# Hybrid encoder trunk on one core: fills stopped in the keys, grouped logarithms, an earlier split of a read-out, whole high parts

## The reference, cut to what matters

```python
xn = rms_norm(x, norm_mix_pre)
ca, cb, cc, cg = split(xn @ w_in)                    # columns of A, B, C and of three gates
h_a = mlstm(ca)                                      # A: matrix memory, 4 heads, chunks
h_b = sliding_window_attention(cb)                   # B: 8 query heads, window 128
h_c = rwkv7(cc)                                      # C: below
g = sigmoid(cg)
merged = g[0] * (h_a @ w_branch_a) + g[1] * (h_b @ w_branch_b) + g[2] * (h_c @ w_branch_c)
x = x + rms_norm(merged @ w_out, norm_mix_post)
gate, up = split(rms_norm(x, norm_ffn_pre) @ w_ffn_in)
x = x + rms_norm((silu(gate) * up) @ w_ffn_out, norm_ffn_post)
```

```python
w = -softplus(-(w0 + tanh(wl) @ w_w2)) - 0.5; decay = exp(-exp(w))
a = sigmoid(a0 + al @ w_a2)
kk = k * k_k / max(sqrt(sum((k * k_k) ** 2)), 1e-12); k = k * (1 + (a - 1) * k_a)
S = S * decay + (S @ -kk) (kk * a)^T + v k^T;  y = S @ r           # token by token
y = (y - mean(y)) * rsqrt(var(y) + GN_EPS) * gn_g + gn_b           # the read-out
y = (y + sum(r * k * r_k) * v) * (sigmoid(gl) @ w_g2)
```

## Time and profile before

| | |
|---|---|
| device time, median of 3 runs | 2463.97 us (2463.54 to 2465.94) |
| the profiled execution | 2466.26 us, its span 2464.5 us |
| granted TensorE clock, mean | 0.976 |
| busy time of TensorE | 2336.3 us (95% of the span) |
| busy time of VectorE | 997.6 us (40%) |
| busy time of ScalarE | 901.3 us (37%) |
| busy time of GpSimd | 786.4 us (32%) |
| table loads on ScalarE | 69, of 1283 ns each, 88.5 us |
| bytes moved | 180.82 MB, mean 73 GB/s |

### The profile page before, as it was taken

How to read it: one execution, slowest core, us unless ns; L and a number is a source line. 1 busy time by engine, 2 the same in 40 slices (tenths; PEclk the granted TensorE clock), 3 DMA queues, 4 the chain that set the end, 5 groups by cost and what they waited for, 6 DMA issues and landing times.

```text
span 2464.5 us, 53615 instructions
## 1 busy us (share of the span) xinstructions
PE 2336.3 (95%) x23450; PEld 2225.3 (90%) x23450; DVE 997.6 (40%) x1559; ACT 901.3 (37%) x1751; POOL 786.4 (32%) x630
## 2 busy tenths in 40 slices
PE   7999989999899899999989999999998989999997
PEld 7998888888789899999989988888887989999997
DVE  4426654455434522320073276545444534332102
ACT  4345532213354522222344455223323444233222
POOL 3332222112235244444324222222112433444441
PEclk9999989999999999999999999999999999999998
DMA  5532211111214132322334221111112242233331
GB/s 162 135 88 65 61 36 32 28 49 32 60 50 143 57 91 86 90 86 86 82 107 130 61 74 48 28 49 32 28 41 63 72 131 61 87 92 89 89 86 52
DMA packets 334193, 180.82 MB, mean 73 GB/s; under 512 B 33528, under 2 KB 330648, under 8 KB 332936
## 3 DMA queue, kind: packets, MB, share of 16 engines
q1 hardware_dynamic: 333776, 177.34, 26.0%
q10 hardware_dynamic: 184, 0.05, 0.0%
HBM read 167.98 MB, written 9.38 MB: 72 GB/s over the span
## 4 chain that ended last, share of the span: by engine, by line
PE 81%; DVE 10%; ACT 4%; issue 3%; DMA 1%; POOL 1%; SPq 0%; DVEq 0%; ACTq 0%; POOLq 0%
PE psum_products L657 72%; PE psum_mixer L657 7%; DMA w_raw<-in_w_in 1%; ACT w_high L1221 1%; DVE xn_low L2047 1%; DVE merged L2041 1%; DVE x L1671 1%; ACT L1221 0%; ACT c_in_rate L1221 0%; DVE squares_ffn L1665 0%; DVE gate_product L2039 0%; POOL w_low L2270 0%; DVE squares L1638 0%; PE psum_mixer L1036 0%; SPq L2118 0%
## 5 line engine op out<-in xcount | busy, mean ns | idle before, releaser
L2270 POOL TENSOR_TENSOR w_low<-w_raw,w_high 128x512 fp32r<-128x512 f32 (+2 forms) x606 | 761.5, 1278 | 1562.4 <-ACT w_high L1221 1561.0
L657 PE MATMUL psum_products<-xn_high,w_high 128*128 128x272 f32 (+1 forms) x3424 | 741.3, 298 | 43.0 <-POOL w_low L2270 14.2
L657 PE MATMUL psum_products<-xn_high,w_low 128*128 128x272 f32 (+1 forms) x3424 | 713.2, 290 | 0.0
L657 PE MATMUL psum_products<-xn_low,w_high 128*128 128x272 f32 (+1 forms) x3424 | 712.1, 290 | 0.0
L657 PEld LDWEIGHTS psum_products<-xn_high,w_high 128*128 128x128 f32 x3424 | 545.1, 190 | 64.2 <-issue 32.8
L657 PEld LDWEIGHTS psum_products<-xn_low,w_high 128*128 128x128 f32 x3424 | 546.1, 191 | 0.0
L657 PEld LDWEIGHTS psum_products<-xn_high,w_low 128*128 128x128 f32 x3424 | 542.8, 191 | 0.0
L1221 ACT ACTIVATE w_high<-w_raw 128x512 fp32r<-128x512 f32 (+2 forms) x606 | 331.2, 595 | 169.8 <-PE psum_products L657 140.1
L657 PE MATMUL psum_products<-hidden_high,w_high 128*128 128x272 f32 x704 | 145.9, 288 | 0.0
L657 PE MATMUL psum_products<-hidden_high,w_low 128*128 128x272 f32 x704 | 145.7, 288 | 0.0
L657 PE MATMUL psum_products<-hidden_low,w_high 128*128 128x272 f32 x704 | 145.1, 288 | 0.0
(11 more groups left out here) (373 smaller groups left out, 2991.7 us busy)
## 6 DMA issues: line engine op xcount, KB each, us to landing
w_raw<-in_w_in SPq DMA_DIRECT2D x112, 512.0 KB, 4.0
w_raw<-in_w_ffn_in SPq DMA_DIRECT2D x88, 512.0 KB, 3.8
w_raw<-in_w_ffn_out SPq DMA_DIRECT2D x32, 512.0 KB, 3.9
w_raw<-in_w_out SPq DMA_DIRECT2D x16, 512.0 KB, 3.9
w_raw<-in_w_ffn_out SPq DMA_DIRECT2D x16, 384.0 KB, 3.3
x_kept<-x SPq DMA_DIRECT2D x2, 2176.0 KB, 7.6
x<-x_kept SPq DMA_DIRECT2D x2, 2176.0 KB, 9.0
w_raw<-in_w_in SPq DMA_DIRECT2D x16, 256.0 KB, 3.8
```

Source lines behind the costliest of these rows:

```text
L657: return pe.matmul(out, lhsT, rhs, start=start, stop=stop, skip_group_check=True)
L2270: low_ready.inc(pool.tensor_tensor(wl[:, n % NSPLIT, ks_], wraw[:, slot, ks_], wh[:, n % NSPLIT, ks_].bitcast(F32), ALU.subtract))
```

## The change

1. `fill` has an argument `on`. With `fill(n, False)` it runs k steps of the next unit only and stops at its end. The three fills of `c_prep`, `c_keys` and `c_scale` are called so. In the plan all units keep their places.
2. The variance step of the read-out writes var with a Copy, and `c_rsqrt` does Ln, two instructions of 128x1090, and then Exp, two of the same size. VectorE's `c_finish` waits at blocks 0 and 2, for one half each.
3. `a_out_split` moves from behind the attention to just ahead of its last step: it now stands between C's column unit 12 and `b_out(8)`.
4. `w_high` is one Copy of up to 128x1024; GpSimd's two subtractions per unit both wait for it.

The diff, cut to its core:

```diff
@@ -163,7 +163,7 @@
 WEIGHT = {"c_prep": 1.0, "c_keys": 1.0, "c_scaled": 0.3, "c_scale": 1.0, "c_gram": 0.7, "c_level": 0.3, "c_chain": 0.5,
-          "c_state_out": 0.0, "a_chunk": 0.6, "a_chunk_out": 0.5, "a_state_out": 0.0, "a_state_put": 0.0, "b_put": 0.0, "c_shift_put": 0.0, "c_state_put": 0.0, "a_scale": 0.3, "a_out": 0.2, "b_values": 0.5,
+          "c_state_out": 0.0, "a_chunk": 0.6, "a_chunk_out": 0.5, "a_out_split": 0.0, "a_state_out": 0.0, "a_state_put": 0.0, "b_put": 0.0, "c_shift_put": 0.0, "c_state_put": 0.0, "a_scale": 0.3, "a_out": 0.2, "b_values": 0.5,
           "b_scores": 0.6, "b_out": 0.6}
@@ -211,13 +211,14 @@
             second += [("b_scores", l, c + 2)] if c < 7 else []
+            second += [("a_out_split", l)] if c == 7 else []
         second = weave(second, [("cols_c", l, j) for j in range(1, CT)])
         plan += second
-        plan += [("a_out_split", l), ("gate", l) + GATES[0], ("c_shift_out", l)]
+        plan += [("gate", l) + GATES[0], ("c_shift_out", l)]
         c = []
@@ -730,10 +731,10 @@
 
-            def fill(steps):
+            def fill(steps, on=True):
 
                 u = unit_at[0]
-                while steps > 0 and u < len(units) and u < unit_at[0] + 2 and fillable(units[u]):
+                while steps > 0 and u < len(units) and u < unit_at[0] + 1 + on and fillable(units[u]):
                     s = units[u]
@@ -822,7 +823,7 @@
 
-                fill(2)
+                fill(2, False)
                 bank[2].claim(pe)
@@ -833,7 +834,7 @@
                 bank[0].filled(to_tokens(0, cc[:, 8:12, at:at + n], nch, L), "act")
-                fill(4)
+                fill(4, False)
 
@@ -846,7 +847,7 @@
             def c_keys(l, g):
-                fill(8)
+                fill(8, False)
 
@@ -1227,8 +1228,8 @@
                 act.wait_ge(landed[at].sem, value)
-                for ks_ in half_blocks(s):
-                    high_ready.inc(fn(wh[:, n % NSPLIT, ks_], wraw[:, unit_no[s] % NRAW, ks_], ACT.Copy))
+                nk = nk_of(s)
+                high_ready.inc(fn(wh[:, n % NSPLIT, 0:nk], wraw[:, unit_no[s] % NRAW, 0:nk], ACT.Copy))
 
@@ -1376,11 +1377,13 @@
                     c0, c1 = (0, Y_CUT) if b == 0 else (Y_CUT, CW)
-                    step(fn(y_rn[:, f, c0:c1], mp[2 + b][:, 0:c1 - c0], ACT.Ln, scale=1.0 / 64, bias=C("scalars", 1, 1)),
-                         bank[2 + b].empty["act"])
+                    step(fn(y_rn[:, f, c0:c1], mp[2 + b][:, 0:c1 - c0], ACT.Copy, scale=1.0 / 64), bank[2 + b].empty["act"])
 
             def c_rsqrt(l):
-                step(fn(y_rn[:], y_rn[:], ACT.Exp, scale=-0.5), flow("c_gn_r"))
+                for f in (0, 2):
+                    step(fn(y_rn[:, f:f + 2, :], y_rn[:, f:f + 2, :], ACT.Ln, bias=C("scalars", 1, 1)))
+                for f in (0, 2):
+                    step(fn(y_rn[:, f:f + 2, :], y_rn[:, f:f + 2, :], ACT.Exp, scale=-0.5), flow("c_gn_r"))
 
@@ -1853,7 +1856,7 @@
 
-                if f == 0:
+                if f % 2 == 0:
                     flow("c_gn_r").wait_next(dve, "dve")
@@ -2266,7 +2269,7 @@
                 for half, ks_ in enumerate(half_blocks(s)):
-                    pool.wait_ge(high_ready.sem, 2 * low_no[n] - 1 + half)
+                    pool.wait_ge(high_ready.sem, low_no[n])
                     low_ready.inc(pool.tensor_tensor(wl[:, n % NSPLIT, ks_], wraw[:, slot, ks_],
```

## The result

| | before | after |
|---|---|---|
| device time, median | 2463.76 us (4 runs, 2462.57 to 2465.94) | 2448.08 us (4 runs, 2445.10 to 2449.73) |
| profiled execution, its span | 2466.26, 2464.5 us | 2449.73, 2447.9 us |
| busy time of TensorE | 2336.3 us | 2335.9 us |
| granted clock, mean of the profiled execution | 0.976 | 0.977 |
| table loads | 69 | 57 |

A forecast was written before the change was run, and what follows sets the result against it. TensorE, busy 95% of the span, bounds the kernel; only its 128 us idle and half-clock time can shrink. Per layer −2.7 + 1.7 − 5.9 + 0 = −6.9; twice, plus 0.5: −13.3 us, so 2450.7 us, range 2437 to 2464.

The forecast's parts named there:

- A: Fills stopping at a unit's end, groups 1 to 4: −2.7 us a layer, +1.7 charged for half clock.
- B: Logarithms grouped in the read-out: fewer table loads and a shorter wait for c_y_squares, −5.9 us a layer.
- C: a_out_split moved inside the attention: new 3.6 us wait against time given back; 0 taken, between −1.5 and +3.5 a layer.
- D: w_high in one Copy: ScalarE wins nothing, GpSimd may begin 0.5 us later; +0.5 us once, at the start.
- 503.4 − 498.4 − 6.0 + 1.5 = +0.5: Group 2: TensorE's arrival less chain end, less eight steps put off, plus two already put off: 0.5 us gained.
- I charge one spell: Waits for c_kprime in groups 1 to 4: one spell of 3.4 us at half clock, costing 1.7 us a layer.
- the three steps put off: Three gate steps now ahead of c_y_squares(1) in the read-out: cut its wait from 0.9 to about 0.4 us.
- that for c_tanh_w shrinks to about 1.2: End of the attention: with the read-out split earlier, TensorE's wait for c_tanh_w shrinks to about 1.2 us.
- But at full clock: Behind the attention: c_tanh_w's matmuls start some 1.6 us later but at full clock, where they took twice their time.
- The first: Rival: the new waits leave the clock alone, −19.7 us, 2444.3 us; chance 0.25.
- The second: Rival: only the table loads count, the other gains go into waits and clock, −1.9 us, 2462 us; chance 0.17.
- the third: Rival: uncovered waits each throw TensorE to 1.2 GHz for 10.2 us, costing 5.1 each; +20.9, 2484.9 us; chance 0.08.

The follow-up runs named there:

- A alone: Only the fills that stop at a unit's end, against the kernel before the change: 2452.02 us, ratio 0.9948.
- C alone: Only the move of a_out_split ahead of the attention's last step, against the kernel before the change: 2468.35 us, ratio 1.0019.
- c_prep only: Only the two fills of c_prep stop at a unit's end, those of c_keys and c_scale go on, against the kernel before the change: 2459.65 us, ratio 0.9982.

## Why the prediction was right, and where it was not

**The total** came out as forecast, but out of terms that were not. Forecast per layer, and measured alone over both layers: A −1.0 with its clock (−2.0 in all), measured −12.8; B −5.9 (−11.8), measured −10.6; C 0, measured +4.7; D +0.5 once, measured +8.4. The measured ones sum to −10.3, where the full change measured −15.3 and −15.7: A and B lose 3 us beside each other, and C and D, which cost 4.7 and 8.4 us alone, cost 5.2 together beside A and B. So the total is right by luck: A was worth far more than forecast, C and D cost what was not forecast, and the parts do not add.

**Part A.** The failed step is "503.4 − 498.4 − 6.0 + 1.5 = +0.5" and its like: it took TensorE's arrival in groups 2 and 4 as fixed, with 2.72 and 3.15 us of waiting for gate_tanh in it. gate_tanh is queued on ScalarE behind the chain that starts 1.5 us sooner, so it came sooner too, and TensorE waits 0.78 and 1.27 us for it after the change. The waits in front of c_kprime came in groups 1 to 3 as forecast, with 1.29, 2.35 and 2.40 us, and not in group 4; new and old together are 8.5 us in layer 0, where some 9 beside 3.4 were forecast. The second failed step is "I charge one spell": A alone ran at a higher clock than before, 0.979. And the three steps put off were credited to B's wait only (0.9 to 0.4), while without B they are worth 2.7 us a layer.

**Part B** held closely: wait 0.8 alone and 0.2 in the full change (0.9 and 0.4 forecast), no wait for c_cols in the finish, −5.3 a layer for −5.9. The load cost 1.28 us with no drain before or behind it: Ln ends at 709.07, the load starts at 709.09, and Exp starts at 710.38, 0.01 us after the load's end. The Trainium skill, "ScalarE: Activation LUTs", section "What ACT_TABLE_LOAD costs", gives 2.66 us for a switch; this trace does not agree.

**Part C.** The wait was forecast (3.6, measured 2.97). The gain set against it was mostly not there: "that for c_tanh_w shrinks to about 1.2" failed, for it is 1.63, held by gate_tanh. "But at full clock" failed in the main: c_tanh_w's own matmuls take 1.51 us in place of 2.04, and those on c_scratch behind them 2.07 as before. So there are two spells and not one, a new one behind the wait for b_probsT_second and the old one somewhat shortened. c_tanh_w stood 3.6 us later than before, not 1.6 (0.7 of it was there before the end of the attention). Alone C cost 2.3 us a layer, between the 0 that was taken and the bound of +3.5; the 0 was chosen, not argued.

**Part D.** The delay of 0.4 us was right. The step that failed is that it reaches TensorE only at the start and in A's chain: it also reaches a_fg, shift_out and VectorE's steps. But with the waits that shrank these come to 0.7 us of idle time in all, and the term put at nothing is the clock, by the estimate 5.7 of the 8.4 us. "In the FFN it hides" was not looked at by itself.

**Rivals.** The first, waits that leave the clock alone, came nearly so for part A: only short spells followed the waits for c_kprime in groups 2 and 3 (0.80 from 572 to 580 us), and groups 1 to 4 as a whole ran at 0.99 after the change, 0.98 before. It did not come for part C. The second, only the table loads count, did not come: A alone gave 12.8 us. Nor did the third, the slower case: the waits in front of c_kprime did not each bring a long stretch at half clock. Its 10.2 us a spell is also more than the 8.4 us of the earlier trace rows.

## What to carry to other kernels

A chain on one engine carries everything queued behind it: when it starts 1.5 us sooner, look for the other waits that end on that engine before the arrival of TensorE, the engine that bounds the kernel, is taken as fixed. A step moved to fill an engine's pause should stand behind what TensorE needs next, not ahead of it: ahead it cost 4.7 us alone, one place later it gained 7.3. A change of some us is best read in two accounts, the idle time and the clock, since here an edit can win in one and lose in the other. And a sum of parts that comes out right shows nothing about the parts: each was run alone here, and the two that were thought nearly free, C and D, each cost time alone.

## What was not expected of the hardware

The mean granted clock of one program varies between executions by up to 0.006 (C alone: 0.973 to 0.979, 2463.3 to 2473.0 us), and with it the time by 10 us, as much as most of these edits. It also moves between programs with nearly the same idle time: c_prep only ran at 0.974 and the whole of A at 0.979 (116.6 and 116.7 us idle). Why is open. And ScalarE's one copy of 1024 saves it 0.1 us (1.04 for 1.13), while the engine behind it starts 0.4 us later.
